# Last expert group of each layer: further rounds ahead of it, no filler products in it, its end and the next norm in halves and tiles

## What is computed

```python
for i in range(2):
    h = rms_norm(x, norm_mix[i]); mkv = mem_n @ w_mem_kv[i]
    if i == 0: mix, mq = neighbourhood attention of h @ na_w_in
    else:      mix, mq = gated linear attention of h @ gla_w_in
    x = x + concat([mix, memory_attention(mq, mkv)]) @ w_out[i]
    x = x + hierarchical_moe(rms_norm(x, norm_ffn[i]), ...)
return rms_norm(x, final_norm)
```

## Time and profile before

| | |
|---|---|
| median of 3 runs | 1258.07 us (1256.88 to 1258.7) |
| the profiled execution | 1258.71 us, its span 1256.9 us |
| bytes read from memory | 442.15 MB |
| TensorE, VectorE, ScalarE busy | 75%, 18%, 12% of the span |
| mean granted TensorE clock | 0.888 of full speed |
| chain that ended last, by engine | PE 60%, DMA 32%, DVE 4%, ACT 2% |

### The profile page before, as it was taken

How to read it: one execution, slowest core, us unless ns; L and a number is a source line. 1 busy time by engine, 2 the same in 40 slices (tenths; PEclk the granted TensorE clock), 3 DMA queues, 4 the chain that set the end, 5 groups by cost and what they waited for, 6 DMA issues and landing times.

```text
span 1256.9 us, 11933 instructions
## 1 busy us (share of the span) xinstructions
PE 944.9 (75%) x5352; PEld 505.1 (40%) x5352; DVE 222.4 (18%) x371; ACT 146.6 (12%) x309; POOL 12.9 (1%) x9
## 2 busy tenths in 40 slices
PE   7999998483968475666999999983847666666666
PEld 5677454141634141313367645541414131323321
DVE  2234141010011010101127321410101010100011
ACT  2233110000000000000124321100000000000001
POOL 0300000000000000000000000000000000000000
PEclk9999999887989696978989999997969697888888
DMA  9982479999999999999983008799999999999992
GB/s 349 278 278 97 171 274 429 428 427 428 429 428 426 430 426 430 427 428 421 321 340 134 1 24 332 317 430 426 429 428 426 430 426 428 428 428 429 425 418 112
DMA packets 77016, 444.05 MB, mean 353 GB/s; under 512 B 31616, under 2 KB 40992, under 8 KB 54304
## 3 DMA queue, kind: packets, MB, share of 16 engines
q1 hardware_dynamic: 76096, 441.31, 86.1%
q10 hardware_dynamic: 864, 1.91, 0.4%
HBM read 442.15 MB, written 1.05 MB: 353 GB/s over the span
## 4 chain that ended last, share of the span: by engine, by line
PE 60%; DMA 32%; DVE 4%; ACT 2%; issue 1%; SPq 0%; DVEq 0%; ACTq 0%
DMA ring<-in_moe_w 32%; PE ps L660 11%; PE ps L656 11%; PE ps L643 8%; PE ps L574 5%; PE ps L610 4%; PE ps L711 4%; PE ps L774 3%; PE ps L835 2%; PE ps L537 1%; ACT work L1026 1%; PE ps L560 1%; PE ps L567 1%; PE ps L583 1%; PE ps L602 1%
## 5 line engine op out<-in xcount | busy, mean ns | idle before, releaser
L656 PE MATMUL ps<-ring,work 128*32 128x512 f32 x2048 | 253.3, 652 | 137.1 <-DMA ring<-in_moe_w 125.7
L660 PE MATMUL ps<-ring,work 128*32 128x512 f32 x1024 | 140.7, 706 | 110.2 <-DMA ring<-in_moe_w 108.8
L656 PEld LDWEIGHTS ps<-ring,work 128*32 128x32 f32 x2048 | 76.6, 119 | 303.0 <-issue 301.4
L643 PEld LDWEIGHTS ps<-work,xs 128*128 128x128 f32 x512 | 124.5, 335 | 6.9 <-issue 3.1
L643 PE MATMUL ps<-work,xs 128*128 128x128 f32 x512 | 123.5, 401 | 1.7 <-DVE work L1322 1.0
L660 PEld LDWEIGHTS ps<-ring,work 128*32 128x32 f32 x1024 | 37.8, 127 | 201.8 <-issue 200.1
L1349 DVE TENSOR_TENSOR xres<-xres,ps 128x1024 f32<-128x1024 f32 x32 | 39.1, 1221 | 341.3 <-PE ps L711 341.3
L711 PE MATMUL ps<-work 128*128 128x512 f32 x128 | 58.7, 602 | 19.5 <-ACT work L1026 19.5
L574 PE MATMUL ps<-ring 128*128 128x384 f32 x192 | 63.7, 489 | 0.0
L610 PE MATMUL ps<-ring 128*128 128x512 f32 x128 | 57.1, 596 | 0.0
L1346 DVE TENSOR_TENSOR work<-work,ps 128x512 f32<-128x512 f32 x16 | 11.0, 688 | 246.4 <-PE ps L656 246.4
(11 more groups left out here) (205 smaller groups left out, 604.5 us busy)
## 6 DMA issues: line engine op xcount, KB each, us to landing
ring<-in_moe_w SPq DMA_DIRECT2D x192, 2048.0 KB, 29.4
ring<-in_w_out SPq DMA_DIRECT2D x4, 2048.0 KB, 13.1
ring<-in_na_w_in SPq DMA_DIRECT2D x6, 1024.0 KB, 11.6
ring<-in_gla_w_in SPq DMA_DIRECT2D x1, 6144.0 KB, 19.4
ring<-in_na_w_in SPq DMA_DIRECT2D x1, 4096.0 KB, 19.7
ring<-in_na_rpb SPq DMA_DIRECT2D x12, 192.0 KB, 5.7
ring<-in_gla_w_in SPq DMA_DIRECT2D x6, 384.0 KB, 4.7
ring<-in_w_mem_kv SPq DMA_DIRECT2D x2, 1024.0 KB, 12.0
```

What stands on the lines that cost most here:

```text
L643: t = pe.matmul(ps[:, k // 4, (k % 4) * P:(k % 4) * P + P], xs[:, a, k::KC], sel[:, a].rearrange("p e s -> p (e s)"), start=a == 0, stop=a ...
L656: return pe.matmul(ps[32 * e:32 * e + 32, 4 + m, :], xsel[:, k, 32 * e:32 * e + 32], w, start=k == 0, stop=k == KC - 1, tile_position=(0, ...
L660: return pe.matmul(ps[32 * e:32 * e + 32, 6 + half, :], actT[:, j, 32 * e:32 * e + 32], w, start=j == 0, stop=j == 3, tile_position=(0, 32 ...
```

## The change

- The branch past the further rounds, with the read of the count, moves on every engine from behind the last quad to ahead of it. Their loop, when entered, works on a copy of the positions (`pposx`) and selects the last quad's rows again afterwards.
- `moe_done` goes. ScalarE's `norm(3)` and `norm(5)`, and GpSimd, wait for counts in `added` instead; TensorE waits for the scaled tiles alone.
- All filler products of the last quads and the six behind layer 0's go. Others stay (`route`, the start).
- In every quad the down product's order becomes half by half where w2 isn't sliced; a new semaphore `down_half` tells that half 0 is done, ScalarE evicts it then, and half 1 as before. The scatter goes half by half, one increment per product, and VectorE adds four times 512 columns instead of twice 1024.
- The norm's mean and epsilon move into ScalarE's root (`bias=eps`, `scale=1/D`), taken for each tile behind its squares. VectorE's scale instruction goes. `tile_scale` takes one tile's reciprocal and then scales that tile. The final norm is `norm(5)`; output tile 0 goes out on SyncE's queue, tile 1 on ScalarE's.

```diff
@@ sync: experts
+                    if g == NQ - 1:
+                        further(l, n0)
...
-                    sp.wait_ge(moe_done[l], 1)
+                    sp.wait_ge(extra_done[l], 1)
...
+            sp.wait_ge(fin_ready, 1)
+            sp.dma_start(out[0, 0:P, :], fin[:, 0, :]).then_inc(s_out, 16)
@@ gpsimd
-            pool.wait_ge(moe_done[0], 1)
+            pool.wait_ge(first.added, NQ * 4)
@@ tensor: quad
                     for j in range(4):
-                        keep_warm(warm, 2)
                         w = landed(8 + j)
                         for half in range(2):
                             for e in range(E4):
                                 o = e * D + half * 512
                                 t = down(j, half, e, w[:, o:o + 512])
+                            if (j, half) == (3, 0):
+                                t.then_inc(rn.sig.down_half, 1)
                         t.then_inc(rn.ring_used, 1)
                 else:
                     ws = [landed(8 + e) for e in range(E4)]
-                    for j in range(4):
-                        for half in range(2):
+                    for half in range(2):
+                        for j in range(4):
...
+                        if half == 0:
+                            t.then_inc(rn.sig.down_half, 1)
-                keep_warm(warm // 2, 2)
                 pe.wait_ge(rn.sig.selwT_ready, c + 1)
-                pe.wait_ge(rn.sig.yb_ready, c * 2 + 2)
-                for a in range(TT):
-                    for half in range(2):
-                        t = pe.matmul(ps[:, 4 + 2 * a + half, :], selwT[:, a, :], yb[:, half * 512:half * 512 + 512],
-                                      start=True, stop=True)
-                    t.then_inc(rn.sig.scattered, 1)
+                for half in range(2):
+                    pe.wait_ge(rn.sig.yb_ready, c * 2 + half + 1)
+                    for a in range(TT):
+                        pe.matmul(ps[:, 4 + 2 * a + half, :], selwT[:, a, :], yb[:, half * 512:half * 512 + 512],
+                                  start=True, stop=True).then_inc(rn.sig.scattered, 1)
@@ tensor: experts
-                if l == 0:
-                    keep_warm(6, 2)
+                    if g == NQ - 1:
+                        further(l)
...
-            pe.wait_ge(moe_done[0], 1)
             transposes(3, xs)
@@ scalar: norm
+                    if i in (3, 5):
+                        act_e.wait_ge(first.added, ((i - 3) // 2 * NQ + NQ - 1) * 4 + 3 + a)
                     nc.scalar.activation(xs[:, a, :], src[:, a, :], ACT.Square,
                                          accum_out=st[:, 2 * i + a:2 * i + a + 1]).then_inc(n_sq, 1)
-                act_e.wait_ge(n_var, i + 1)
-                nc.scalar.activation(st[:, 24 + 2 * i:26 + 2 * i], st[:, 12 + 2 * i:14 + 2 * i], ACT.Sqrt).then_inc(n_sd, 1)
+                    act_e.wait_ge(n_sq, TT * i + a + 1)
+                    nc.scalar.activation(st[:, 24 + 2 * i + a:25 + 2 * i + a], st[:, 2 * i + a:2 * i + a + 1], ACT.Sqrt,
+                                         bias=eps[:, 0:1], scale=1.0 / D).then_inc(n_sd, 1)
@@ scalar: quad
-                act_e.wait_ge(rn.ring_used, rn.used(pair, n0 + 12))
                 for half in range(2):
+                    if half == 0:
+                        act_e.wait_ge(rn.sig.down_half, c + 1)
+                    else:
+                        act_e.wait_ge(rn.ring_used, rn.used(pair, n0 + 12))
                     nc.scalar.copy(yb[:, half * 512:half * 512 + 512], ps[:, 6 + half, :]).then_inc(rn.sig.yb_ready, 1)
@@ vector: quad, tile_scale
+                for half in range(2):
+                    for a in range(TT):
+                        cols = xres[:, a, half * 512:half * 512 + 512]
+                        dve.wait_ge(rn.sig.scattered, c * 4 + (2 * half + a + 1))
+                        V.tensor_tensor(cols, cols, ps[:, 4 + 2 * a + half, :], ALU.add).then_inc(rn.sig.added, 1)
...
+            def tile_scale(i, a):
+
+                dve.wait_ge(n_sd, TT * i + a + 1)
+                r = st[:, 48 + 2 * i + a:49 + 2 * i + a]
+                link(V.reciprocal(r, st[:, 24 + 2 * i + a:25 + 2 * i + a]))
+                return r
...
-                V.tensor_copy(ntmp[:, 0:1], xres[:, 0, 0:1]).then_inc(moe_done[l], 1)
```

More of the change, by code:

```diff
@@ L107, in build @@
         roundf = sb("roundf", [P, 1])
+        eps = sb("eps", [P, 1])
         work = sb("work", [P, 5120])
@@ L188, in build @@
         ntmp = cut(work, 5048, 2)
+        pposx = cut(work, 4600, TT, NE + E4)
         mem_tokens = cut(ring, 9 * SLOT + 2048, TT, D)
@@ L433, in load, with further @@
                 sp.dma_start(dst, src).then_inc(rn.ring_in[slot], 16)
[L435 to L443, removed]
+            def further(l, n0):
                 sp.wait_ge(rt_n[l], 1)
@@ L455, in experts @@
                                     load(extra, slot, l, pair * 2 + s, f, ())
-                    sp.wait_ge(moe_done[l], 1)
+                    sp.wait_ge(extra_done[l], 1)
                     sp.sem_inc(sp_spare, 1)
+            def experts(l):
+                for g in range(NQ):
+                    n0 = first_fill(l, g)
+                    if g == NQ - 1:
+                        further(l, n0)
+                    if l == 0 and g == KV_AT:
+                        free(0, n0 - 1)
+                        sp.dma_start(kvw[1], rows(w_mem_kv[1], 0, 512)).then_inc(ring_in[kv_slot], 16)
+                    for f in range(FILLS):
+                        free(l, n0 + f)
+                        load(main[l], main[l].slots[n0 + f], l, g, f, SLICED[g])
             sp.sem_inc(more_used, XSLOTS)
@@ L731, in experts @@
                                      r * SELS + pair * 4 + (2 * s + 1))
+                    pe.wait_ge(again[l], 2)
+            def experts(l):
+                for g in range(NQ):
+                    if l == 0 and g == KV_AT:
+                        mem_kv(1)
+                        pe.wait_ge(kv_cp[1], 2)
+                    if g == NQ - 1:
+                        further(l)
+                    quad(main[l], l * NQ + g, 0, first_fill(l, g), l * SELS + 2 * g + 1, SLICED[g])
             def v_na(p):
@@ L1039, in experts @@
                                 quad(extra, r * NQ + pair * 2 + s, r * PAIRS + pair, s * FILLS)
+                    act_e.wait_ge(extra_done[l], 1)
+            def experts(l):
+                for g in range(NQ):
+                    if l == 0 and g == KV_AT:
+                        copy_kv(1)
+                    if g == NQ - 1:
+                        further(l)
+                    quad(main[l], l * NQ + g, 0, first_fill(l, g))
             act_e.wait_ge(s_scrap, 1)
             table(ACT.Sqrt)
+            act_e.wait_ge(s_eps, 1)
             act_e.wait_ge(s_mem, 16)
@@ L1346, in quad, with further @@
                 V.tensor_tensor(act, sg, ps[:, 5, :], ALU.mult).then_inc(rn.sig.act_ready, 1)
[L1347 to L1351 removed]
+                for half in range(2):
[3 more added lines that the diff above has]
+                        V.tensor_tensor(cols, cols, ps[:, 4 + 2 * a + half, :], ALU.add).then_inc(rn.sig.added, 1)
+                dve.wait_ge(rn.sig.added, c * 4 + 4)
+            def further(l):
+                dve.wait_ge(rt_n[l], 1)
+                lo, hi = rounds(dve, l)
+                with dve.If(hi > lo):
+                    V.tensor_copy(pposx, ppos).then_inc(pos_saved[l], 1)
+                    dve.wait_ge(pos_saved[l], 1)
+                    with dve.Fori(lo, hi) as r:
+                        V.tensor_scalar(pposx, pposx, -float(CAP), None, ALU.add).then_inc(next_round, 1)
+                        dve.wait_ge(next_round, r + 1)
+                        select(pposx, more.sel_ready, 0)
+                        select_w(more.sel_ready, 0, r * SELS + 1)
+                        with dve.Fori(0, PAIRS) as pair:
+                            for s in range(2):
+                                quad(extra, l, r * NQ + pair * 2 + s, r * PAIRS + pair, s * FILLS, pair * 2 + s,
+                                     r * SELS + pair * 4 + (2 + 2 * s), pposx)
+                    select(ppos, again[l], NQ - 1)
+                    select_w(again[l], NQ - 1, 1)
+                    V.memset(scrap[:, 0:1], 1.0).then_inc(extra_done[l], 1)
             def experts(l):
[L1354 removed]
+                select(ppos, first.sel_ready, 0)
                 dve.wait_ge(rt_p[l], 2)
```

98 lines of the change are left out of this document (29 added, 69 removed).

## The result

The changed kernel took 1248.83 us, the median of 20 executions (1241.11 to 1257.62), beside 1257.88 of the kernel before (20 executions, 1254.19 to 1260.22). The ratio is 0.9936 [0.9914, 0.9958]: 8.0 us faster by the ratio (the two medians lie 9.05 apart), about half of the 15.9 that was forecast, and inside the range. But the median describes no execution. The 20 times form two groups with nothing between them: ten at 1241.11 to 1244.07, around the forecast 1242.2, and ten at 1253.59 to 1257.62. The median is the midpoint between 1244.07 and 1253.59, and one more execution in either group would have moved it by almost 5; that it lies inside the range is luck. The kernel before ran 106 times beside all kernels of this study and never took more than 1260.73; it has one group.

What follows compares the result with a forecast made beforehand. Weight traffic bounds the middle of the expert stages, so only layer ends can gain. 4.2 + 4.9 + 4.8 + 5.0 = 18.9, less 3.0 for the clock, is 15.9: from 1258.71 to 1242.8, median 1242.2; range 1238.5 to 1249.5.

Steps and rivals of the forecast that it cites:

- What bounds, and where a gain can lie: Expert stages: weight traffic at 425 to 430 GB/s bounds middle quads; gains only at layer ends and in layer 1's mixing.
- Fillers removed, 4.2 and 4.8: Last quads: without fillers the last down step starts at its weights' landing, gaining 4.2 in layer 0, 4.8 in layer 1.
- The end by halves and the norm by tiles: Behind the last down step's end, T: first projection at T + 10.0, span's end at T + 11.15; gains 4.9 and 5.0.
- The branch, nothing: Last quads: the moved branch, 4.45 and 3.43 on TensorE, is covered by waits for weights and costs nothing up to 12.4.
- The rival of the fetch waiting behind the queued weights: Moved branch: instruction fetch queues behind all weight loads, 23.5 a branch; 1264 at the least, chance 0.05.
- The clock's 3.0 at the three gaps: Waits before both last steps and after layer 0's scatter: one and a half clock falls cost 3.0, bounds 0 and 6.9.
- So I carry the whole 4.2 + 4.9 through to the end: Layer 0 into layer 1: layer 0's gains pass undiminished through layer 1's mixing, a TensorE chain with little traffic.
- the clock pays in full: Rival: clock falls at all three gaps and narrow first projections stay slow; gain 9.5, 1248.6, chance 0.10.

Runs made afterwards that it cites:

- ag_fill: a_gap1 with all filler products of the last quads and the six behind layer 0's put back; 1248.58 us, ratio 0.9936.
- ag_best: ag_pool with two filler products ahead of the last down step and two behind layer 0's experts; 1240.65 us, ratio 0.9869.
- after_again: The changed kernel run once more, unedited, to see its share of late executions; 9 of 12 late, ratio 0.997.
- a_gap1: The changed kernel with one filler product in the 0.66 us wait ahead of layer 1's narrow output products; 1241.9 us, ratio 0.9885.
- ag_pool: a_gap1 with GpSimd's resets of a layer 1 buffer waiting for layer 1's first projection, not layer 0's last add; 1241.22 us, ratio 0.9869.
- bg_nofill: The kernel before plus one filler ahead of layer 1's output products, without the last quads' fillers and layer 0's six; 1253.3 us, ratio 0.9973.

## Why the prediction was half right

- **What bounds, and where a gain can lie**: right. Traffic in the middle is unchanged.
- **Fillers removed, 4.2 and 4.8**: right. The last steps start 0.05 behind their landings. Less its share of the clock the forecast gives 6.0 (4.2 + 4.8 - 3.0), and ag_fill measures 6.7.
- **The end by halves and the norm by tiles**: the middle was right, with the squares at T + 3.54 for 3.65 and the first root's end at T + 5.02 for 5.05. From T to the first projection 11.55, not 10.0: scaling 1.46 for 0.71, beside the memset that the adds released, and sixteen transpose records at 1.2 GHz, 3.42, of which eight took 1.17 in ag_best at 2.4 GHz. From T to the end 11.1 for 11.15.
- **The branch, nothing**: right, about 0.8, within the scatter. Much of its cover was spent, though: TensorE stood 4.20 and 5.21 ahead of the gather, and its wait for w3 shrank to 5.75 and 5.24. The rival of the fetch waiting behind the queued weights, 23.5 a branch, falls.
- **The clock's 3.0 at the three gaps**: the three were mostly low. The steps lost 1.45 and 1.5 and the transposes 1.1, 4.1 together. But the first projection came 5.8 earlier and the output stage 9.1: in between the kernel before had lost 3.3 that the changed one did not (its fall at 648.5, above). The net is near 1, and by the output stage the whole 9.1 was there. One reading under it is off: granted 0.62 in 1208 to 1209 puts that fall at about 1208.2, 4.5 behind the stop and not 4.9; it changes nothing.
- **The step that failed** is "So I carry the whole 4.2 + 4.9 through to the end", and with it the clock's term. I counted the falls at the gaps that the change makes, and took layer 1's mixing as a chain of fixed length. It isn't: it has a stage of narrow products that runs in 17.6 or in 29.6, and the change, without touching it, moved the moment at which it begins. In 19 of 32 executions this costs 12.0 + 1.9 = 13.9. The term should have read: 3.0 for the gaps, and 13.9 times the share of late executions, as a mean. With 10 in 20 that is 7, and 1242.2 + 7 = 1249.2, for a mean of 1249.24. No row of the kernel before gives that share.
- The rival "the clock pays in full" gave nearly the measured time, 1248.6, by another way: in the profiled late execution the first projections were at 2.4 GHz, and the loss lay 95 us later. In after_again they were slow in part (5.53 for 3.64), as that rival says, and that execution took 1245.02. The number is no support for it.

Shown: the place of the loss and its size, and that the same program goes both ways. Supported by counts: that a small delay ahead of the stage changes the share of late executions (17 in 23 to 1 in 6, and 19 in 32 to none in 13 over three delays). Not shown: that filling the short wait averts the fall by itself, since the filler also delays; no late one in 62 is in its favour, and the fall at line 826 without a wait is against it. Open: which starting moments fall, why the kernel before has none in 106, the 1414.38, and why two products didn't hold the clock ahead of layer 0's last step.

The change with the filler of a_gap1 and the later memset, ag_pool, beats both kernels: 0.9869 of before, 16 us, with no late one in its 4 executions.

## What to carry to other kernels

A forecast by the length of a chain assumes that the pieces behind the change keep their durations. If a stage behind it consists of narrow products after a short wait, look whether it could run at the lower clock, price that, and expect two groups of times. Both outcomes have to stand in the forecast, since the profile of one execution shows only one of them. Look at the single times ahead of the median, and before crediting a 0.4 us edit with 14 us, run the unedited kernel often enough to know its share. Where such a stage starts with a wait, one full product in it cost nothing here; whether it is the cure was not isolated. When removing fillers, fit the work around the hole together: the same removal was worth 3.3 with the scatter behind a gap, where layer 0's ran at 1.2 GHz in the profile of bg_nofill (5.65 for 3.69), and 6.7 with the scatter straight behind the step.

## What the runs showed that was not expected

- TensorE fell to 1.2 GHz while busy without a pause, 2.6 to 2.9 us behind the start of 64 x 192 and 96 x 192 products, and over 23 us more of them did not bring 2.4 GHz back; the full-width products of line 621 did, at about 757. The Trainium skill ("TensorE: Matmul & The Clock Gate", Why this matters for your kernels) warns of idle gaps between bursts; here the gap was 0.66, and the products behind it narrow; in the kernel before the clock fell 2.8 behind the start of the 32 x 256 products of line 826 with no gap at all.
- A 96 x 2048 memset on GpSimd nearly doubled a 128 x 1024 scaling on VectorE (0.75 to 1.46), and two memsets of 96 x 16 took 0.55 and 0.53 beside the next scaling, 0.12 alone.
- A branch on TensorE under full traffic left 4.20 and 5.21 us without a product.
